# Tokens 256 to 519 of a hybrid decoder step: gates, z, GLU, branch a, xBC and convolution move into the expert steps of tokens 0 to 255

## What is computed

```python
h = modulate(rmsnorm(x, g_norm1), sh1, sc1)
proj = h @ w_in                       # u 512 | z 1024 | xBC 2048 | dt 16 | gates 2 x 1024
ya, sr, si = s5_branch(u, ...)        # complex diagonal scan, GLU: y * sigmoid(y @ w_glu + b_glu)
yb, nbuf, hl = mamba2_branch(z, xbc, dt, ...)   # causal conv of 4 taps, silu, SSD in chunks of 128, gated norm
merged = gates[:, :D] * (ya @ w_branch_a) + gates[:, D:] * (yb @ w_branch_b)
x = x + gt1 * (merged @ w_out)
h2 = modulate(rmsnorm(x, g_norm2), sh2, sc2)
x = x + gt2 * peer(h2, w_query, sub_keys, expert_down, expert_up)
```

## Time and profile before

| | us |
|---|---|
| median of 3 runs | 2325.96 |
| lowest and highest | 2323.35, 2326.16 |
| the profiled execution, its own time | 2322.33 |
| its span, first to last instruction | 2320.6 |
| begin of `stage_s5`, `stage_ssd`, `stage_query`, `stage_peer` in the span | 113.2, 508.5, 744.8, 809.4 |
| first gather of steps 0, 6, 11, 16, 25, 29 | 823.1, 935.0, 1067.8, 1171.4, 1387.4, 1482.9 |

### The profile page before, as it was taken

One profiled execution on the slowest core, in us unless ns is written; L12 is line 12 of the kernel. 1 busy time (PEld: TensorE's weight loads), 2 busy tenths in 40 slices (PEclk: granted clock), 3 DMA queues, 4 the chain that ended last, 5 costly groups with the idle time before them and its releaser, 6 DMA issues.

```text
span 2320.6 us, 20282 instructions
## 1 busy us (share of the span) xinstructions
PE 1297.8 (56%) x6476; PEld 764.4 (33%) x6476; DVE 1453.9 (63%) x3416; ACT 338.5 (15%) x782; POOL 1043.2 (45%) x1124
## 2 busy tenths in 40 slices
PE   4597998799966745444538858533232433222234
PEld 0176765568855433212315535300000000000000
DVE  0344899317533279677996685567866786776740
ACT  1011000102230122112310121100101011110100
POOL 0014000000000045665775576567775777777764
PEclk8798999799978877757768979756655755656666
DMA  9821210211111489999999999999998999999987
GB/s 367 325 88 37 73 37 1 84 51 39 43 69 55 162 311 386 411 409 357 406 407 408 408 410 410 405 410 400 411 412 319 405 403 411 411 412 411 411 353 284
DMA packets 226789, 673.63 MB, mean 290 GB/s; under 512 B 26380, under 2 KB 69036, under 8 KB 222544
## 3 DMA queue, kind: packets, MB, share of 16 engines
q0 software_dynamic: 149760, 545.33, 58.9%
q1 hardware_dynamic: 76098, 125.31, 14.8%
q10 hardware_dynamic: 824, 1.70, 0.2%
HBM read 663.24 MB, written 9.15 MB: 290 GB/s over the span
## 4 chain that ended last, share of the span: by engine, by line
DMA 24%; POOL 12%; DVE 11%; issue 8%; PE 7%; DVEq 1%; ACT 1%; SPq 0%; POOLq 0%; ACTq 0%
DMA arena<-in_expert_up_dram,rows 10%; POOL arena L1768 6%; POOL arena L1748 6%; DMA out_dram<-arena 5%; DVE arena L2186 5%; DMA arena<-in_expert_down_dram,expert 5%; PE ps L1952 3%; PE ps L1298 1%; PE ps L2048 1%; PE ps L2061 1%; DMA arena<-in_w_branch_b_dram 1%; DMA arena<-in_w_out_dram 1%; DMA arena<-in_w_query_dram 1%; PE ps L1960 1%; DMA arena<-in_state_ssm_dram 1%
## 5 line engine op out<-in xcount | busy, mean ns | idle before, releaser
L1952 PE MATMUL ps<-arena 128*32 128x512 f32 x2048 | 376.7, 869 | 724.8 <-DMA arena<-in_expert_up_dram,rows 724.7
L2186 DVE CUSTOM_DVE_ANT_0 arena<-arena,ps 128x1024 f32<-128x1024 f32 x512 | 609.2, 1217 | 224.0 <-DMA arena<-in_expert_down_dram,expert 214.6
L1768 POOL DMA_INDIRECT arena<-in_expert_up_dram,rows x512 | 488.2, 954 | 250.2 <-issue 142.7
L1748 POOL DMA_INDIRECT arena<-in_expert_down_dram,expert x512 | 489.3, 956 | 238.1 <-issue 141.9
L1952 PEld LDWEIGHTS ps<-arena 128*32 128x32 f32 x2048 | 77.9, 138 | 963.0 <-issue 962.3
L590 PE MATMUL ps<-arena 128*128 128x264 f32 x896 | 209.4, 392 | 15.0 <-PEq L2412 6.9
L590 PEld LDWEIGHTS ps<-arena 128*128 128x128 f32 x896 | 171.3, 193 | 55.7 <-issue 16.2
L956 POOL MEMSET arena<- 128x528 f32 x2 | 1.1, 538 | 307.8 <-POOLq L2412 307.7
L1298 PE MATMUL ps<-arena 128*128 128x256 f32 (+1 forms) x512 | 126.3, 409 | 9.1 <-DMA arena<-in_w_query_dram 4.9
L1788 ACT ACTIVATE arena<-arena 128x8 f32<-128x8 f32 x65 | 13.5, 208 | 769.9 <-DVE arena L2186 769.7
L1055 PE MATMUL ps<-arena 128*128 128x264 f32 x512 | 114.4, 385 | 0.0
(11 more groups left out here) (416 smaller groups left out, 1948.1 us busy)
## 6 DMA issues: line engine op xcount, KB each, us to landing
arena<-in_w_ada_dram SPq DMA_DIRECT2D x12, 2048.0 KB, 20.0
arena<-in_w_in_dram SPq DMA_DIRECT2D x11, 2048.0 KB, 8.6
arena<-in_w_query_dram SPq DMA_DIRECT2D x16, 1024.0 KB, 16.3
arena<-in_w_ada_final_dram SPq DMA_DIRECT2D x4, 2048.0 KB, 17.1
arena<-in_w_out_dram SPq DMA_DIRECT2D x8, 1024.0 KB, 17.1
arena<-in_expert_down_dram,expert POOLq DMA_INDIRECT x512, 11.5
arena<-in_expert_up_dram,rows POOLq DMA_INDIRECT x512, 11.4
out_dram<-arena SPq DMA_DIRECT2D x13, 512.0 KB, 24.7
```

The source lines that it names most:

```text
L1748: G.indirect_dma_start(U[i], None, down, bass.IndirectOffsetOnAxis(ap=at, axis=0))\
L1768: G.indirect_dma_start(Vr[r][j], None, up, bass.IndirectOffsetOnAxis(ap=at, axis=0))\
L1952: last = mm(ps[32 * j:32 * j + 32, c, :], Z[:, j, m, :], Vr[r][4 * half + j][:, c * 512:(c + 1) * 512], start=(p % 4 == 0 and m == 0), sto ...
L2186: V.tensor_tensor_reduce(U[i], U[i], row, 1.0, 0.0, ALU.mult, ALU.add, dots[n % 2][:, j:j + 1]).then_inc(s_uused, 1)
```

## The change

- hT is split into hA (tokens 0 to 255) and hB (256 to 519). `stage_s5` becomes `stage_mix`: only the 4 tiles of u and the dt projection take all tokens. Gate b, xBC (16 tiles), gate a and z are made for tokens 0 to 255, one matmul of 256 a k, banks 5 and 6 in turn. 24 tiles stand ahead of the scan loop, 2 in each of its first 10 iterations. dt, softplus and cumulative sums move from `stage_ssd` ahead of the scan tables. B's sparse layout is smaller (4 POOL copies, 8 transposes), gelu is applied within the loop for both halves.
- Behind the loop, the convolution of tokens 0 to 255 (ScalarE the first tap, VectorE three) is mixed with GLU and branch a of the same tokens.
- `stage_ssd` keeps the chunks 0 and 1, norm and branch b.
- `stage_peer`: `front()` gets the xBC tiles of hB and their convolution, the sample tokens' convolution, the transposes of B and C and of the tails with their stores, GLU, gate a, branch a, z and gate b of hB. Its weights come through the same ring of two pieces, in one list `order` of 46 pieces (45 loaded in the stage). TensorE's slots become 74. All engines now pass three slots a step (none in the sample step). The samples' states start behind the xBC work, a sample every second slot.

```diff
-                nc.scalar.activation(hT[:, 4 * half:4 * half + 4, b * P:b * P + m],
+                dst, at = (hA, b * P) if b < 2 else (hB, (b - 2) * P)
+                nc.scalar.activation(dst[:, 4 * half:4 * half + 4, at:at + m],
...
+    tiles = [("u", i) for i in range(4)] + [("gB", i) for i in range(KD)] + [("x", i) for i in range(NCV)] \
+        + [("gA", i) for i in range(KD)] + [("z", i) for i in range(KD)]
...
+    EARLY = 24
...
+                    if i == 0:
+                        mm(ps[:, 5, 0:HA], w, hA[:, k, 0:HA], start=(k == 0), stop=(k == KD - 1))
+                        last = mm(ps[:, 6, 0:HW], w, hB[:, k, :], start=(k == 0), stop=(k == KD - 1))
+                    else:
+                        last = mm(ps[:, 5 + n % 2, 0:HA], w, hA[:, k, 0:HA], start=(k == 0), stop=(k == KD - 1))
...
+            for m in range(4):
                 for k in range(4):
-                    for h in range(2):
-                        last = nc.tensor.matmul(ps[:, 2 * (m % 2) + h, 0:HW], glu_w[:, k, m * P:(m + 1) * P],
-                                                yg[:, k, span(h)], start=(k == 0), stop=(k == 3))
+                    last = mm(ps[:, m, 0:HA], glu_w[:, k, m * P:(m + 1) * P], yg[:, k, :], start=(k == 0), stop=(k == 3))
...
+    order = ([("q", 1), ("x", 0), ("x", 1), ("x", 2), ("q", 2), ("x", 3), ("x", 4), ("x", 5), ("q", 3), ("x", 6), ("x", 7)]
+             + [("q", h) for h in range(4, PH)] + [("glu", 0), ("gA", 0), ("gA", 1), ("bra", 0), ("gA", 2), ("gA", 3), ("bra", 1)]
+             + [("z", i) for i in range(4)] + [("gB", 0), ("gB", 1), ("brb", 0), ("gB", 2), ("brb", 1), ("gB", 3), ("brb", 2),
+                                               ("brb", 3)] + [("wo", i) for i in range(4)] + [("Q", h) for h in range(PH)])
...
+                if p >= 2:
+                    sp.wait_ge(t_mm, last_of(*order[p - 2]))
+                s = slot(name, i)
+                sp.dma_start((Q.ring if n == 256 else ring4)[s], rows_of(w)[:, :, c0 + n * i:c0 + n * i + n]).then_inc(t_w[s], 16)
...
+            load(15)
+            load(16)
+            load(17)
             for b in range(NS):
-                if b < 4:
-                    load(3 + b)
                 sample(b)
-                if b == 5:
-                    load(7)
-                    load(8)
+                if b == 0:
+                    load(18)
+                    load(19)
+                elif b == 1:
+                    load(20)
...
+                if g != S:
+                    next(late, None)
+                    next(late, None)
                 if n >= LAG:
                     add(n - LAG, 0)
-                next(late, None)
+                if g != S:
+                    next(late, None)
```

More of the change, by code:

```diff
@@ L161, in __init__ @@
         self.ys_s = take(KD, NS)
+        self.hist = take(NCV, 24)
+        self.carry = take(NCV, 3)
         assert M <= Map.SCR
@@ L566, in _ @@
+            act.wait_ge(s_carry, 1)
+            for n in range(4):
+                tap(n)
+            act.wait_ge(s_ysamp, 4)
+            S.activation(ygB[:, :, HA:HW], ygB[:, :, HA:HW], ACT.Gelu).then_inc(s_gelu, 1)
+            for n in range(4, 8):
+                tap(n)
+            for n in range(4):
+                silu(n)
             for m in range(4):
@@ L665, in _ @@
             y(NS5 - 1)
-            while n < NP:
-                proj(n)
-                n += 1
+            pe.wait_ge(s_dta, 2)
+            pe.wait_ge(s_pev, NP)
+            for c in range(NB):
+                nc.tensor.transpose(ps[:, 5, c * 32:c * 32 + 16], csv[:, chunk(c)], ident[0:NH, 0:NH])
+                nc.tensor.transpose(ps[:, 5, c * 32 + 16:c * 32 + 32], dtk[:, chunk(c)], ident[0:NH, 0:NH])
+            pe.wait_ge(s_dexp, 3)
+            pe.wait_ge(s_ek, 1)
+            for k in range(KD):
+                last = mm(ps[:, 5, 128 + 17 * k:145 + 17 * k], ek[:, k, :], rex, start=True, stop=True)
+            last.then_inc(s_tmps, 1)
             pe.wait_ge(s_new, 1)
@@ L1507, in stage_peer @@
     stat3, rstd3 = take(3), take(3)
+    tail = take(NCV, 11)
+    bglu = take(4)
+    bgn = take(P, rows=4)
     assert M <= Map.W, M
@@ L1853, in front @@
                 SE.activation(sq, cv[:, 0:KD, :], ACT.Square).then_inc(t_sq, 1)
+                act.wait_ge(t_tlw, 32)
+                for j in range(2):
+                    sigmoid("gB", 0, j, j)
                 yield from pause(3)
@@ new lines, in front @@
+                pe.wait_ge(t_ssilu, 1)
+                for j in range(8):
+                    last = nc.tensor.transpose(ps[0:NS, 2 + j // 4, (j % 4) * P:(j % 4 + 1) * P], cv[:, 8 + j, HA:HW], ident)
+                last.then_inc(t_bcps, 1)
+                yield
+                pe.wait_ge(t_bcs, 2)
+                both("q", 6, Q.h2T, HA)
+                yield
+                score(6)
+                both("q", 7, Q.h2T, HA)
+                yield
+                score(7)
+                pe.wait_ge(t_srd, PH - 1)
@@ new lines, in front @@
+                acc = cv[:, :, HA:HW]
+                dve.wait_ge(t_gone, gone["x", 7, 1])
+                dve.drain()
+                done(tt(acc, taps[0], wide8[0], ALU.mult))
+                done(tt(acc, acc, wide8[4], ALU.add))
+                for j in (1, 2, 3):
+                    done(tt(some8, taps[j], wide8[j], ALU.mult))
+                    last = tt(acc, acc, some8, ALU.add)
+                    if j < 3:
+                        done(last)
+                last.then_inc(t_sconv, 1)
@@ new lines, in front @@
+                sample(1)
+                yield
+                for i in range(2):
+                    for j in range(4):
+                        added("bra", i, j, j)
+                        if j == 1:
+                            yield
+                    sample(2 + 2 * i)
+                    yield from pause(2)
+                    sample(3 + 2 * i)
+                    yield
+                yield
+                sample(6)
+                yield from pause(2)
+                sample(7)
```

1197 lines of the change are left out of this document (681 added, 516 removed).

## The result

The changed kernel takes 2309.9 us in the median of 4 runs (2307.88 to 2311.27), the kernel before 2325.93 us beside it; the ratio is 0.9934 with an interval of [0.9923, 0.9946]. So it is faster, by 16 us (0.7%) where 96 were forecast. The profiled execution has a span of 2307.4 us, 13.2 less than before.

A forecast was written before the change was run, and what follows sets the result against it. A TensorE and VectorE chain was taken to bound the kernel up to 809.4 us, the DMA engines the expert stage after it. -190 ahead and +95 there make -95 from 2325.96, say 2230 us; range 2185 to 2295 us.

The forecast's parts named there:

- The work ahead of the experts: Stages ahead of the expert stage: it starts 190 us earlier, bounds 175 and 196.
- the bound of 90: Expert stage: POOL's wait for TensorE's adds exceeds 90 us and stands in steps 6 to 10 and 17 to 24.
- taken +95: Expert stage, steps 0 to 28: added pieces and stalled gathers lengthen it; stretches sum to +99, taken as +95 us.
- The DMA engines are the bound: Expert stage, from 809.4 us: DMA engines set the time, most slices at 400 to 412 GB/s, so added bytes lengthen it.
- 37 us: Expert stage: three slots with pieces a step, at 12.2 us each with full queues, make 37 us.
- +9 for such a stretch: Expert stage, steps 11 to 15: chunk halves at 3 slots a step instead of 2 cost +9 us.
- -14 for the bare steps behind it: Expert stage, steps 25 to 28: nothing late is left, 82 us instead of 95.5, so -14 us.
- Both fit, if their waits shrink.: Expert stage: added 29 us on VectorE's 503 and some 168 us on TensorE's 386, of 673, fit.
- not 59: Expert stage: 24.1 MB of added weight pieces at 409 GB/s cost 59 us, the lower bound.
- slots pace steps 4 to 24: Rival, expert stage: samples at saturated landing and three-piece steps at 35 us; +150, 2286 us, chance 0.20.
- the one I gave 0.06: Rival, expert stage: slots keep their mean of 11.6 us, 74 last 858 us; slower, +77, 2403 us, chance 0.06.
- decides from a mean slot of 10.6 us upwards: Expert stage: mean slot length from which the slower-than-before rival (chance 0.06) decides, 10.6 us.

The follow-up runs named there:

- e9_halfup: Changed kernel with half of every expert_up row gathered (2 KB instead of 4), same number of gathers: 2236.8 us.
- e5_before3: Kernel before with nothing moved, its 56 late slots passed three a step instead of two: 2380.3 us, ratio 1.0217.
- e3_spread: Changed kernel with all its work, but five late slots in two steps instead of six: 2328.8 us.
- e10_deep: Changed kernel with half of every expert_up row gathered and the freed halves making the up ring two steps deep: 2196.7 us.

## Why the prediction was wrong

**What held.** The work ahead of the experts was costed right: 190 forecast, 193.3 measured, within its bounds; chunk work from 457.9 us (461), query from 551.0 (555), experts from 616.1 (620). The loop started at 232.6 (233) and its iterations stood 11.2 us apart, every fourth 11.6, one 13.7. Timeline, VectorE, the loop's first products:

```profile
232.57 0.69 DVE L907 TENSOR_TENSOR arena<-ps,arena 128x512 f32<-128x512 f32 x1 [11.28 <-PE ps L712]
...
243.73 0.69 DVE L907 TENSOR_TENSOR arena<-ps,arena 128x512 f32<-128x512 f32 x1
...
403.97 0.69 DVE L907 TENSOR_TENSOR arena<-ps,arena 128x512 f32<-128x512 f32 x1
```

Late work ended in step 25, nothing of it ran at step 32, and from there to the end the time changed by -2.7 us (764.8 against 767.5). GpSimd's wait for TensorE stood where it was forecast (92.2 us in steps 6 to 10, 98.7 in 16 to 24), but at 238.4 us in all it was far more than the bound of 90 that the forecast gave it.

**What failed** is the one term "taken +95" for steps 0 to 28; it measured +190.2. By its own stretches:

| steps | forecast | measured |
|---|---|---|
| 0 to 5 | +16 | +36.6 |
| 6 to 10 | +52 | +64.5 |
| 11 to 15 | +9 | +28.9 |
| 16 to 24 | +36 | +71.5 |
| 25 to 28 | -14 | -11.3 |

All stretches with late work were forecast too short, and three steps of the argument made them so.

- **The bound.** "The DMA engines are the bound", read from 400 to 412 GB/s, led to stretches costed as bytes at 409 GB/s plus a little. e9_halfup shows that bare steps are set by GpSimd's 16 issues, 19.9 us. For bytes alone this changes little. It matters because GpSimd is one engine with one order: a time in which it waits can't be made up later by faster transfers. The prediction had the number that fits steps with three pieces, 37 us, and let it go for the bytes: it took steps 16 to 24 at 252/9 = 28 us each, and six of the nine measured 33.6 to 38.8.
- **The pace.** The third slot of a step was priced at almost nothing for work that was there before: the table had +9 for such a stretch, and -14 for the bare steps behind it. e5_before3 prices it at 53 us (62 at step 29) with nothing moved.
- **"Both fit, if their waits shrink."** TensorE's busy time rose by 183.5 us (168 forecast) to 569.5 of 863.7. I compared sums over the stage. But between GpSimd and TensorE lies a ring one step deep, so the comparison must be made step by step: with three pieces 26 us against 19.9, and the slack of a light step can't be lent to a heavy one.

**Bytes** were a smaller part. By the queue shares of 616 to 1480 and of 809 to 1483 us, SP's queue took 0.229 x 864 = 198 us for 66.4 MB against 0.171 x 674 = 115 for 39.6, so 3.1 us per MB for what was added, where the gathers took 0.667 x 864/223 = 2.6. At 24.1 MB that is some 74 us and not 59 of the DMA engines' time. The Trainium skill ("Perfetto Trace Analysis", section "DMA Optimizations") says that small DMAs, under 2 KB, carry a significant overhead per transfer. The pieces move rows of 1 KB, the gathers 4 KB, and the trace agrees, with 3.1 against 2.6 us per MB, though the two also differ in their queue, and no run separates that from the size of a row. But taking most of those bytes away gave only 30 us.

**The rivals.** By the time, "slots pace steps 4 to 24" (0.20, 2286 us) came nearest: it had the right steps and +150, 40 too little. By the mechanism the one I gave 0.06 belongs beside it: slots keep their mean of 11.6 us and the kernel is slower (2403 us), and it "decides from a mean slot of 10.6 us upwards". The measured mean is (863.7 - 82)/74 = 10.6 us, the very point at which front and experts cancel. My argument against it, that the old mean came from the bytes of a step and not from the slots, holds only in part: pressed to three a step, unchanged work took 9.3 us a slot (521.6/56 in e5_before3), less than 11.6, but more than the 7.9 that the bytes of that stretch (348 GB/s over 521.6 us) need at 409 GB/s, and gathers waited for the slots.

**How far the cause is settled.** Shown, at step 29: 62 us of packing (in the kernel before), 62 for half of the added arithmetic and 7/8 of the added bytes together, 39 that the ring's depth alone gives back (with half rows), 25 for split pieces, 23 for the states. These overlap, and are no sum. The round GpSimd, down rows, VectorE's slot, TensorE's slot, additions, GpSimd is shown by the timeline of e3_spread, and by e10_deep, where opening it at one place moves the wait to the next. Not shown is what the late chain would take with VectorE's slots out of the way of its products; orders that put them elsewhere were not run. Not shown either is what steps 16 to 24 would take at two slots a step in the old order; their +71 us is the largest open part.

## What to carry to other kernels

Before work is moved beside a saturated stage, compare the engines step by step and not by their sums over the stage, wherever the ring between them is only a step deep; a step costs at least the longest engine's work in it, and a bare step gives nothing back. Price the pace by itself, as a change apart from the work that it carries: run the old work at the new pace. When a load is taken away as a test, look at which stretch got shorter: here nearly all of the gain stood in one, and the largest loss in another. And where several engines share one hand-made order, look for the closed round (who waits for whom until it comes back to the first), since taking load off one of them then yields only a part.

## What was not expected of the hardware

- A row gather of 128 rows costs GpSimd 1.24 us of issuing, whether rows have 4 KB or 2 KB: the shortest steps of 16 gathers took 19.9 us in both kernels, at 404 and 309 GB/s in the mean of steps 32 to 63. The Trainium skill ("DMA: Bandwidth & Descriptors", section "Issuing engines are not separate DMA queues") calls the sequencer's time to initiate a DMA usually small relative to the DMA itself; here it is as long as the transfer (by estimate, 0.524 MB at 413 GB/s are 1.27 us) and sets the least length of a step, so the measurement decides. The Trainium skill ("Perfetto Trace Analysis", section "DMA Optimizations") names generation of descriptors as a possible bottleneck. The trace agrees so far that GpSimd is busy with these instructions one behind another (0.94 us, 0.30 us, and so on); what it does within them the trace doesn't show.
- With up rows of 2 KB the landings of both kinds fell to less than two thirds, and steps 32 to 63 together got only 2% shorter. DMA issues, 1543 to 1900 us of the changed kernel:

```profile
arena<-in_expert_down_dram,expert POOLq DMA_INDIRECT x128, 9.6
arena<-in_expert_up_dram,rows POOLq DMA_INDIRECT x122, 11.0
```

and 1600 to 1900 us of e9_halfup:

```profile
arena<-in_expert_down_dram,expert POOLq DMA_INDIRECT x110, 6.0
arena<-in_expert_up_dram,rows POOLq DMA_INDIRECT x104, 4.0
```
